# Cutting the A22 weight block last: a reordered weight preparation in a seven-product matmul pipeline

## The chip, the cores and the metric

One core of one Trainium2 chip. The metric is the device time of one execution in microseconds. The kernel runs from instruction streams written out by hand for TensorE (PE), VectorE (DVE), ScalarE (ACT), GpSimd (POOL) and SyncE (SP), which meet only at semaphores; each engine takes its own instructions strictly in order.

## The reference

Two decoder layers over 1024 tokens of width 1024, in float32. Layer 0: RMSNorm with shift and scale from `c`, a gated mixer, a squared-ReLU MLP of width 4096, then one shared key/value projection. Layer 1: stick-breaking attention with 16 heads, then a second MLP.

```python
uv = gelu(h @ w_in); u, v = split(uv); v = _rmsnorm(v, v_norm_g)   # w_in: 1024 x 4096
z = einsum("gts,bnsgc->bntgc", tril(w_s), v) + b_s                 # per chunk of 128 tokens
y = (u * z) @ w_out
...
y = jnp.square(jax.nn.relu(h @ mlp_w_up[layer])) @ mlp_w_down[layer]   # 1024 x 4096, 4096 x 1024
```

Three of these matmuls have the shape (1024 tokens x 1024) by (1024 x 4096): `h @ w_in` and `h @ mlp_w_up` of both layers. The change is about them. They are called stage 0, 1 and 2 below.

## The kernel before

Activations lie transposed, channels on the 128 partitions and tokens along the row. To keep float32 accuracy every operand is kept as two parts in the PE's reduced float format: a high part (`HI`, a copy made by ACT) and a low part (`LO`, the difference, made by DVE). A matmul is then three (`three`, lines 2091 to 2093). Making these two parts is called cutting.

**A stage.** The first 4 of the 32 output tiles (128 channels each) are computed plainly (units `plain`). The other 28 go in 14 pairs of two tiles (`PAIRS`). One pair is a 2 x 2 block matmul (contraction split in two, tokens split in two) done with 7 products in place of 8. The blocks of a pair's weights are

- A1: the upper-left and lower-left quarter together, 128x1024 per cut,
- A22: one quarter, 128x512, read by the seventh product only,
- S1, S2, S3, S4: sums and differences of quarters, 128x512 each, made by `weight_sums` on DVE (lines 1609 to 1614).

The four token blocks T1 to T4 (`T_RAW`, `T_HI`, `T_LO`) are made once per stage. PE runs the products of a pair in the order A1, A1, S2, S1, S3, S4, A22, 12 matmuls of 128x512 each. ACT keeps the first product (`keep`), DVE combines the products: c11 (2 additions, after the third product), c22 (3, after the fifth), c12 (1, after the sixth) and c21 (1, after the seventh), all line 1629. PE waits for c11 before its seventh product, because that one goes to the bank of the third, and for c21 of the pair before at its third product (`made(0)`).

**The pipeline.** While PE works on pair p, ACT and DVE cut the weights of pair p+1 into the other of two weight buffers (`WX`/`WY` for even pairs, `W` for odd ones). The raw weights of one pair lie in a single buffer `RAW` of two 512 KB tiles. SP loads the next pair into it (`load_pair`, line 556) once DVE has counted off the pair's A22 cut. Semaphore `w_lo` counts the cuts in the order of the numbers at line 32 (A1 0, A22 1, S2 2, S1 3, S3 4, S4 5), and every engine's code must cut in that order.

SP's queue also carries, in program order, the stores of the four finished outputs of a pair (`store`, each waits for ACT to finish it) and the loads of modulation weights (`load_mod`, `MODRAW`, 512 KB), each of which waits until DVE has reduced the one before (`mod_reduce`, line 405). Stage 0 has one reduction in each of its first 6 pairs (which also have four additions for a norm, `add_v`), and three or fewer in the others; stage 1 has two in even pairs and one in odd ones; stage 2 has none. At the end of stage 0 the spatial weights `WS_RAW` are loaded; POOL masks them, ACT and DVE cut them in the last pair.

## Time and profile before

| | us |
|---|---|
| median of 3 runs (range) | 2572.84 (2570.56 to 2576.83) |
| the profiled execution, its own time | 2572.84 |
| its span on the engines | 2571.1 |
| PE busy in the span | 2513.3 |
| DVE busy | 1583.1 |
| ACT busy | 995.7 |
| DMA queue q1, share of 16 engines | 41.4% |

1.7 us of the execution lie outside the span. The granted clock of the TensorE was 0.997 on average. A busy time is a union of intervals; matmuls overlap, so a matmul of 390 ns is followed by the next after about 227 ns (12 matmuls, one product, in 2.72 us).

### The profile page before, as it was taken

The numbers are of one execution on the slowest core, as the hardware profiler recorded it, in microseconds if no ns is written. First come the engines' busy times: TensorE is split into PE (matmuls) and PEld (weight loads), VectorE is DVE, ScalarE is ACT, GpSimd is POOL, SyncE is SP. The second block draws the span as 40 slices with busy tenths as digits, with TensorE's granted clock in tenths as the row PEclk, the third lists the DMA queues.
The fourth block names the chain that finished last, engine by engine and source line by source line (L and its number), as shares of the span: only waits on it lengthen the run. The fifth ranks groups of instructions, "written<-read, shape, count | busy, mean of one in ns | idle before, by whom it ended". The sixth has DMA issues, their size and how long they took to land.

```text
span 2571.1 us, 33672 instructions
## 1 busy us (share of the span) xinstructions
PE 2513.3 (98%) x12220; PEld 2053.6 (80%) x12220; DVE 1583.1 (62%) x1907; ACT 995.7 (39%) x1429; POOL 148.9 (6%) x155
## 2 busy tenths in 40 slices
PE   6999999999999999999999999999999999999999
PEld 4888888888888878888898887665788888888887
DVE  6878776668876666666633545777258655444442
ACT  5553343236444431111311335777236444311110
POOL 0000000000000000000000003665000000000000
PEclk9999999999999999999999999999999999999999
DMA  6335573213444475554142264654322322632311
GB/s 255 127 135 180 189 263 121 99 58 126 161 159 151 172 279 185 187 199 139 43 158 82 95 180 131 138 122 113 119 107 107 117 104 106 253 123 82 114 49 66
DMA packets 122981, 359.61 MB, mean 140 GB/s; under 512 B 12032, under 2 KB 28416, under 8 KB 118912
## 3 DMA queue, kind: packets, MB, share of 16 engines
q1 hardware_dynamic: 122880, 358.23, 41.4%
q8 instruction: 67, 1.10, 0.2%
q14 instruction: 34, 0.28, 0.0%
HBM read 270.10 MB, written 88.08 MB: 139 GB/s over the span
## 4 chain that ended last, share of the span: by engine, by line
PE 87%; DVE 6%; ACT 3%; DMA 2%; issue 1%; SPq 0%; ACTq 0%; DVEq 0%
PE PS L2091 25%; PE PS L2092 25%; PE PS L2093 25%; DVE KEEP L2012 2%; PE PS L2612 2%; PE PS L2597 2%; PE PS L2195 1%; PE PS L2197 1%; PE PS L2196 1%; PE PS L2577 1%; PE PS L2498 1%; ACT PS L1314 1%; PE PS L2578 1%; DVE T_RAW L1597 1%; DVE T_LO L1602 1%
## 5 line engine op out<-in xcount | busy, mean ns | idle before, releaser
L2091 PE MATMUL PS<-HID_HI,W_HI 128*128 128x512 f32 x1024 | 400.1, 391 | 5.4 <-DVE HID_LO L1648 5.0
L2093 PE MATMUL PS<-HID_HI,W_LO 128*128 128x512 f32 x1024 | 398.5, 389 | 0.0
L2092 PE MATMUL PS<-HID_LO,W_HI 128*128 128x512 f32 x1024 | 398.4, 389 | 0.0
L395 ACT ACTIVATE W_HI<-RAW 128x1024 fp32r<-128x1024 f32 x114 | 119.5, 1059 | 615.7 <-PE PS L2093 509.6
L1494 DVE SCALAR_TENSOR_TENSOR X<-PS,MODV,X 128x1024 f32<-128x1024 f32 x124 | 159.1, 1283 | 284.0 <-PE PS L2093 275.5
L2091 PE MATMUL PS<-H_HI,W_HI 128*128 128x512 f32 x700 | 277.6, 397 | 4.0 <-DVE H_LO L1438 2.8
L2093 PE MATMUL PS<-H_HI,W_LO 128*128 128x512 f32 x700 | 273.6, 391 | 0.0
L2092 PE MATMUL PS<-H_LO,W_HI 128*128 128x512 f32 x700 | 273.2, 390 | 0.0
L2091 PEld LDWEIGHTS PS<-HID_HI,W_HI 128*128 128x128 f32 x1024 | 192.2, 188 | 49.9 <-DVE HID_LO L1648 7.9
L2093 PEld LDWEIGHTS PS<-HID_HI,W_LO 128*128 128x128 f32 x1024 | 192.2, 188 | 40.0
L2092 PEld LDWEIGHTS PS<-HID_LO,W_HI 128*128 128x128 f32 x1024 | 192.2, 188 | 39.5 <-issue 0.2
L2012 DVE TENSOR_TENSOR_SCAN KEEP<-PS,MASK 128x1024 f32<-128x1024 f32 (+3 forms) x112 | 147.6, 1349 | 47.1 <-ACT PS L1314 38.0
L399 DVE TENSOR_TENSOR W_LO<-RAW,W_HI 128x1024 fp32r<-128x1024 f32 x124 | 150.1, 1218 | 41.7 <-ACT W_HI L1112 24.6
L2091 PEld LDWEIGHTS PS<-H_HI,W_HI 128*128 128x128 f32 x700 | 131.9, 188 | 33.9 <-DVE H_LO L1438 4.3
L405 DVE SCALAR_TENSOR_TENSOR MODRAW<-MODRAW,PS 128x1024 f32<-128x1024 f32 x96 | 116.7, 1216 | 62.4 <-DMA MODRAW<-in_modw 62.1
L2093 PEld LDWEIGHTS PS<-H_HI,W_LO 128*128 128x128 f32 x700 | 131.7, 188 | 28.4
L2092 PEld LDWEIGHTS PS<-H_LO,W_HI 128*128 128x128 f32 x700 | 132.0, 189 | 26.6 <-issue 0.5
L2091 PE MATMUL PS<-T_HI,W_HI 128*128 128x512 f32 x336 | 130.9, 390 | 0.0
L897 POOL TENSOR_TENSOR A<-KEEP 128x1024 f32<-128x1024 f32 (+3 forms) x112 | 126.3, 1147 | 78.6 <-DVE KEEP L2012 77.6
L2093 PE MATMUL PS<-T_HI,W_LO 128*128 128x512 f32 x336 | 130.7, 389 | 0.0
L2092 PE MATMUL PS<-T_LO,W_HI 128*128 128x512 f32 x336 | 130.7, 389 | 0.0
L1629 DVE TENSOR_TENSOR TN<-PS,TN 128x512 f32<-128x512 f32 x147 | 101.3, 689 | 43.2 <-PE PS L2093 38.1
(234 smaller groups left out, 4952.9 us busy)
## 6 DMA issues: line engine op xcount, KB each, us to landing
RAW<-in_wt SPq DMA_DIRECT2D x208, 512.0 KB, 4.0
MODRAW<-in_modw SPq DMA_DIRECT2D x96, 512.0 KB, 3.5
HRAW<-hid_scratch SPq DMA_DIRECT2D x14, 2048.0 KB, 9.1
hid_scratch<-TN SPq DMA_DIRECT2D x90, 256.0 KB, 2.2
hid_scratch<-SCR SPq DMA_DIRECT2D x84, 256.0 KB, 2.2
x_scratch<-X SPq DMA_DIRECT2D x3, 4096.0 KB, 13.8
X<-x_scratch SPq DMA_DIRECT2D x6, 2048.0 KB, 9.2
QK<-qk_scratch SPq DMA_DIRECT2D x16, 768.0 KB, 6.3
```

Of the source, the lines that this page charges most:

```text
L395: act.activation(ring_view(W_HI, n), raw_view(n), ACT.Copy).then_inc(sem["w_hi"], 1)
L399: dve.tensor_tensor(ring_view(W_LO, n), raw_view(n), ring_view(W_HI, n).bitcast(F32), ALU.subtract).then_inc(sem["w_lo"], 1)
L405: dve.scalar_tensor_tensor(MODRAW[:], MODRAW[:], 1.0, flat(CROW), ALU.mult, ALU.mult, accum_out=MODA[:, bass.ds(m.v, 1)]).then_inc(sem["mo ...
L897: pool.tensor_tensor(A[b][:, STRIP[t]:STRIP[t] + w], KEEP[k % 4][:, 0:w], KEEP[k % 4][:, 1:w + 1], ALU.subtract).then_inc(sem["a_ok"], 1)
L1494: dve.scalar_tensor_tensor(X[:, k, :], flat(acc(u % 2)), MODV[:, gate + k:gate + k + 1], X[:, k, :], ALU.mult, ALU.add).then_inc(sem["acc_ ...
L1629: dve.tensor_tensor(HS[x][:, c, :], PS[:, bank, :], HS[x][:, a, :], ALU.add).then_inc(sem["c_made"], 1)
L2012: dve.tensor_tensor_scan(KEEP[k % 4][:, 1:1 + w], strip_scores(k, w), MASK[:, 0:w], 1.0, ALU.mult, ALU.max).then_inc(sem["scanned"], 1)
L2091: pe.matmul(dst, w_hi, m_hi, start=first, stop=False)
L2092: pe.matmul(dst, w_hi, m_lo, start=False, stop=False)
L2093: return pe.matmul(dst, w_lo, m_hi, start=False, stop=last)
L2597: mm = pe.transpose(PS[:, TURNED[n % 3], m * P:(m + 1) * P], block, IDENT[:])
L2612: pe.matmul(PS[r, 6, 0:w], VH[:, b, j, r], AT[q % 3 * 2 + x][:, 0:w], start=(j == KT - 1), stop=(j == 4 * g)).then_inc(sem["av_done"], 1)
```

## The change

The A22 block becomes the last in the cutting order, on ACT, DVE and in the count. Beside that:

- `load_pair`, which waits for the A22 cut, moves down in SP's code: behind the first store and one or two `load_mod` of the pair.
- In a stage's first pair DVE does c11 first, and cuts S2, S1, S3, S4 and A22 only after c21. In the second pair c11 comes ahead of the A1 cut. In all later pairs A22 is cut between S4 and c12.
- `WS_RAW` gets another place (the memory of the even pairs' A22 cut), and is loaded in the next-to-last pair after the seventh product, not at its start.
- In stage 0's last kind of pair one `load_mod` moves ahead of the last store.

```diff
-A1, A22, S2, S1, S3, S4 = range(BLOCKS)
+A1, S2, S1, S3, S4, A22 = range(BLOCKS)
...
-        WS_RAW = at("WS_RAW", [P, GROUPS, CHUNK], F32, RC)
+        WS_RAW = at("WS_RAW", [P, GROUPS, CHUNK], F32, RX + 24 * KB)
...
@@ SP, stages 1 and 2
                 def pair(p, x):
-                    load_pair(p + 1)
                     store(p, 0, 0, 0, 0)
                     if mods:
                         load_mod(sp, p // 2 * 3 + GMODS + 1 + 2 * x)
+                    load_pair(p + 1)
                     if mods and x == 0:
                         load_mod(sp, p // 2 * 3 + GMODS + 2)
...
@@ SP, stage 0
                 def v_pair(p):
-                    load_pair(p + 1)
                     store(p, 0, 0, 0, 0)
                     load_mod(sp, p + 1)
+                    load_pair(p + 1)
                     stores(p)
...
                 def u_pair(p, mods):
-                    load_pair(p + 1)
                     store(p, 0, 0, 0, 0)
                     for n in range(1, min(mods, 2) + 1):
                         load_mod(sp, first + n)
+                    load_pair(p + 1)
                     store(p, 2, 0, 1, 1)
                     store(p, 3, 1, 2, 0)
-                    store(p, None, 1, 3, 1)
                     if mods > 2:
                         load_mod(sp, first + 3)
+                    store(p, None, 1, 3, 1)
...
@@ SP, stage 0, next-to-last pair
                 p = Count(PAIRS - 2)
-                sp.wait_ge(sem["mod_red"], GMODS)
-                sp.dma_start(WS_RAW[:], spw).then_inc(sem["spw_in"], 16)
+                store(p, 0, 0, 0, 0)
                 load_pair(p + 1)
-                store(p, 0, 0, 0, 0)
...
                 store(p, 2, 0, 1, 1)
+                sp.wait_ge(sem["product"], count_of(0, p, PRODUCTS, 7).v)
+                sp.dma_start(WS_RAW[:], spw).then_inc(sem["spw_in"], 16)
...
@@ ACT, start of stages 1 and 2 (of stage 0 and on DVE alike)
                 block_cut(Count(0), 0, A1)
-                block_cut(Count(0), 0, A22)
                 plain(2)
-                for b in (S2, S1, S3, S4):
+                for b in (S2, S1, S3, S4, A22):
                     block_cut(Count(0), 0, b)
...
@@ DVE, pair
+                    second = p.i is None and p.c == 1
+                    if second:
+                        c11(p, x)
                     block_cut(p + 1, 1 - x, A1)
                     weight_sums(p + 1, 1 - x)
-                    block_cut(p + 1, 1 - x, A22)
...
-                    c11(p, x)
+                    if not second:
+                        c11(p, x)
...
                     block_cut(p + 1, 1 - x, S4)
+                    block_cut(p + 1, 1 - x, A22)
                     if kind == "v":
                         add_v(p, 1)
                     c12(p, x)
...
@@ DVE
                 def first_pair():
                     p = Count(0)
+                    c11(p, 0)
                     block_cut(p + 1, 1, A1)
                     weight_sums(p + 1, 1)
-                    block_cut(p + 1, 1, A22)
-                    c11(p, 0)
-                    for b in (S2, S1, S3):
-                        block_cut(p + 1, 1, b)
                     c22(p, 0)
-                    block_cut(p + 1, 1, S4)
                     c12(p, 0)
                     c21(p, 0)
+                    for b in (S2, S1, S3, S4, A22):
+                        block_cut(p + 1, 1, b)
```

DVE, first pair of stage 1, before. `W_LO<-RAW` with 8x128 is the A1 cut and with 4x128 the A22 cut, `S_RAW<-` the sums, `W_LO<-S_RAW` the S cuts, `SCR<-PS,SCR` the combinations of this pair:

```order
L1621 TENSOR_TENSOR W_LO<-RAW,W_HI 128x8x128
L1609 TENSOR_TENSOR S_RAW_107<-RAW 128x4x128
L1610 TENSOR_TENSOR S_RAW_107<-RAW 128x4x128
L1612 TENSOR_TENSOR S_RAW_107<-S_RAW_107,RAW 128x4x128
L1614 TENSOR_TENSOR S_RAW_107<-RAW,S_RAW_107 128x4x128
L1621 TENSOR_TENSOR W_LO<-RAW,W_HI 128x4x128
L1629 TENSOR_TENSOR SCR<-PS,SCR 128x512 x2
L1621 TENSOR_TENSOR W_LO<-S_RAW_107,W_HI 128x4x128 x3
L1629 TENSOR_TENSOR SCR<-PS,SCR 128x512 x3
L1621 TENSOR_TENSOR W_LO<-S_RAW_107,W_HI 128x4x128
L1629 TENSOR_TENSOR SCR<-PS,SCR 128x512 x2
L405 SCALAR_TENSOR_TENSOR MODRAW,MODA<-MODRAW,PS 128x1024 x2
```

The same place in the changed kernel:

```order
L1627 TENSOR_TENSOR SCR<-PS,SCR 128x512 x2
L1619 TENSOR_TENSOR W_LO<-RAW,W_HI 128x8x128
L1607 TENSOR_TENSOR S_RAW_107<-RAW 128x4x128
L1608 TENSOR_TENSOR S_RAW_107<-RAW 128x4x128
L1610 TENSOR_TENSOR S_RAW_107<-S_RAW_107,RAW 128x4x128
L1612 TENSOR_TENSOR S_RAW_107<-RAW,S_RAW_107 128x4x128
L1627 TENSOR_TENSOR SCR<-PS,SCR 128x512 x5
L1619 TENSOR_TENSOR W_LO<-S_RAW_107,W_HI 128x4x128 x4
L1619 TENSOR_TENSOR W_LO<-RAW,W_HI 128x4x128
L405 SCALAR_TENSOR_TENSOR MODRAW,MODA<-MODRAW,PS 128x1024 x2
```

Of the seven additions of the combinations the two of c11 now stand ahead of the A1 cut and the five of c22, c12 and c21 ahead of the S cuts, and the A22 cut stands last, with the modulation reductions still behind it.

DVE, second pair of stage 1, before (`TN<-PS,TN` are its combinations):

```order
L1621 TENSOR_TENSOR WX_LO<-RAW,WX_HI 128x8x128
L1609 TENSOR_TENSOR S_RAW_106<-RAW 128x4x128
L1610 TENSOR_TENSOR S_RAW_106<-RAW 128x4x128
L1612 TENSOR_TENSOR S_RAW_106<-S_RAW_106,RAW 128x4x128
L1614 TENSOR_TENSOR S_RAW_106<-RAW,S_RAW_106 128x4x128
L1621 TENSOR_TENSOR WY_LO<-RAW,WY_HI 128x512
L1629 TENSOR_TENSOR TN<-PS,TN 128x512 x2
L405 SCALAR_TENSOR_TENSOR MODRAW,MODA<-MODRAW,PS 128x1024
L1621 TENSOR_TENSOR WX_LO<-S_RAW_106,WX_HI 128x4x128 x3
L1629 TENSOR_TENSOR TN<-PS,TN 128x512 x3
L1621 TENSOR_TENSOR WX_LO<-S_RAW_106,WX_HI 128x4x128
L1629 TENSOR_TENSOR TN<-PS,TN 128x512 x2
```

And in the changed kernel:

```order
L1627 TENSOR_TENSOR TN<-PS,TN 128x512 x2
L1619 TENSOR_TENSOR WX_LO<-RAW,WX_HI 128x8x128
L1607 TENSOR_TENSOR S_RAW_106<-RAW 128x4x128
L1608 TENSOR_TENSOR S_RAW_106<-RAW 128x4x128
L1610 TENSOR_TENSOR S_RAW_106<-S_RAW_106,RAW 128x4x128
L1612 TENSOR_TENSOR S_RAW_106<-RAW,S_RAW_106 128x4x128
L405 SCALAR_TENSOR_TENSOR MODRAW,MODA<-MODRAW,PS 128x1024
L1619 TENSOR_TENSOR WX_LO<-S_RAW_106,WX_HI 128x4x128 x3
L1627 TENSOR_TENSOR TN<-PS,TN 128x512 x3
L1619 TENSOR_TENSOR WX_LO<-S_RAW_106,WX_HI 128x4x128
L1619 TENSOR_TENSOR WY_LO<-RAW,WY_HI 128x512
L1627 TENSOR_TENSOR TN<-PS,TN 128x512 x2
```

c11 has moved to the front, and the A22 cut (`WY_LO<-RAW`) from behind the sums to behind the S4 cut.

SP, the next-to-last pair of stage 1, before:

```order
L556 DMA RAW<-in_wt 128x1024 x2
L550 DMA hid_scratch<-SCR 128x512
L387 DMA MODRAW<-in_modw 128x1024 x2
L550 DMA hid_scratch<-SCR 128x512 x3
L587 DMA HRAWX<-hid_scratch 128x4x1024
```

And in the changed kernel:

```order
L550 DMA hid_scratch<-SCR 128x512
L387 DMA MODRAW<-in_modw 128x1024
L556 DMA RAW<-in_wt 128x1024 x2
L387 DMA MODRAW<-in_modw 128x1024
L550 DMA hid_scratch<-SCR 128x512 x3
L587 DMA HRAWX<-hid_scratch 128x4x1024
```

The two weight loads stand behind the first store and one modulation load, and ahead of the second modulation load.

## Rows read from the trace of the kernel before

**Rows 1.** Page, part 1: busy us (share of span) and instructions of each engine.
```profile
PE 2513.3 (98%) x12220; PEld 2053.6 (80%) x12220; DVE 1583.1 (62%) x1907; ACT 995.7 (39%) x1429; POOL 148.9 (6%) x155
```

**Rows 2.** Waits of PE, whole span: us in total, times, longest.
```profile
PE PS L2101 <- DVE TOT L1411: 20.1, 1, 20.1
...
PE PS L2091 <- DVE HID_LO L1648: 5.0, 7, 1.6
...
PE PS L2091 <- DVE SCR L1629: 0.8, 2, 0.4
```

**Rows 3.** Stretches: us long, then busy us (x instructions) of each engine, clock, DMA.
```profile
97.00:130.00 33.00, 33.00 (x147) 27.35 (x146) 29.25 (x44) 15.29 (x25) 0.00 (x0) 1.00 0.41 138
```

**Rows 4.** Timeline of PE: start us, us, engine, line, op, [idle before <-releaser].
```profile
90.20 0.39 PE L2091 MATMUL PS<-H_HI,WX_HI 128*128 128x512 f32 x1
...
637.42 0.39 PE L2091 MATMUL PS<-H_HI,WX_HI 128*128 128x512 f32 x1
...
654.29 0.47 PE L2091 MATMUL PS<-T_HI,WY_HI 128*128 128x512 f32 x1 [0.39 <-DVE SCR L1629]
```

**Rows 5.** Timeline of SP, second block.
```profile
856.56 0.90 SPq L556 DMA_DIRECT2D RAW<-in_wt  x2
...
875.51 0.83 SPq L556 DMA_DIRECT2D RAW<-in_wt  x2
```

**Rows 6.** Timeline of DVE, second block, first pair.
```profile
630.52 0.69 DVE L1621 TENSOR_TENSOR WY_LO<-RAW,WY_HI 128x512 fp32r<-128x512 f32 x1
...
646.99 2.29 DVE L1602 TENSOR_TENSOR T_LO<-T_RAW,T_HI 128x2048 fp32r<-128x2048 f32 x1
649.19 1.22 DVE L1621 TENSOR_TENSOR W_LO<-RAW,W_HI 128x1024 fp32r<-128x1024 f32 x1
...
653.46 1.48 DVE L1629 TENSOR_TENSOR SCR<-PS,SCR 128x512 f32<-128x512 f32 x2
...
656.66 2.27 DVE L1629 TENSOR_TENSOR SCR<-PS,SCR 128x512 f32<-128x512 f32 x3
...
665.81 1.22 DVE L405 SCALAR_TENSOR_TENSOR MODRAW<-MODRAW,PS 128x1024 f32<-128x1024 f32 x1 [3.75 <-DMA MODRAW<-in_modw]
```

**Rows 7.** Timeline of DVE, first block, first pair.
```profile
96.54 2.29 DVE L1602 TENSOR_TENSOR T_LO<-T_RAW,T_HI 128x2048 fp32r<-128x2048 f32 x1 [2.03 <-ACT T_HI L1035]
```

**Rows 8.** Timelines of DVE and ACT, second block, a late pair.
```profile
871.12 1.22 DVE L1621 TENSOR_TENSOR W_LO<-RAW,W_HI 128x1024 fp32r<-128x1024 f32 x1 [3.66 <-ACT W_HI L1045]
...
880.37 2.29 DVE L1629 TENSOR_TENSOR SCR<-PS,SCR 128x512 f32<-128x512 f32 x3 [0.54 <-PE PS L2093]
883.26 1.22 DVE L405 SCALAR_TENSOR_TENSOR MODRAW<-MODRAW,PS 128x1024 f32<-128x1024 f32 x1 [0.61 <-DMA MODRAW<-in_modw]
...
870.04 1.57 ACT L1045 ACTIVATE W_HI<-RAW 128x1024 fp32r<-128x1024 f32 x2
```

**Rows 9.** DMA to landing: weight loads all, those at 642, modulation rows 93 to 345.
```profile
DMA to landing us min/median/max: 3.2/4.0/5.5
...
DMA to landing us min/median/max: 4.8/5.2/5.5
...
DMA to landing us min/median/max: 3.2/3.5/4.4
```

**Rows 10.** Stretches after two PE waits, and the first of the waits.
```profile
60.00:63.50 3.50, 3.50 (x10) 2.67 (x10) 2.78 (x5) 3.06 (x5) 0.00 (x0) 0.54 0.00 0
...
953.00:957.00 4.00, 2.47 (x11) 2.05 (x12) 4.00 (x6) 0.00 (x0) 0.00 (x0) 1.00 0.55 155
...
PE PS L2091 <- DVE H_LO L1438: 2.2, 1, 2.2
```

**Rows 11.** Timelines of SP, POOL and ACT around the gate weights.
```profile
321.69 0.34 SPq L679 DMA_DIRECT2D WS_RAW<-in_spw  x1
...
325.35 1.09 POOL L859 TENSOR_SCALAR_AFFINE_SELECT WS_RAW<-WS_RAW 128x1024 f32<-128x1024 f32 x1 [323.01 <-DMA WS_RAW<-in_spw]
...
348.89 1.04 ACT L1206 ACTIVATE H_HI<-WS_RAW 128x1024 fp32r<-128x1024 f32 x1
```

More of the change, by code:

```diff
@@ L1175, in mixer @@
                 block_cut(Count(0), 0, A1)
-                block_cut(Count(0), 0, A22)
                 t_cut(1, 4)
@@ L1179, in mixer @@
                 t_cut(2, 5)
-                for b in (S2, S1, S3, S4):
+                for b in (S2, S1, S3, S4, A22):
                     block_cut(Count(0), 0, b)
@@ L1726, in first_pair @@
                     p = Count(0)
+                    c11(p, 0)
                     block_cut(p + 1, 1, A1)
                     weight_sums(p + 1, 1)
-                    block_cut(p + 1, 1, A22)
-                    c11(p, 0)
-                    for b in (S2, S1, S3):
-                        block_cut(p + 1, 1, b)
                     c22(p, 0)
-                    block_cut(p + 1, 1, S4)
                     c12(p, 0)
                     c21(p, 0)
+                    for b in (S2, S1, S3, S4, A22):
+                        block_cut(p + 1, 1, b)
                     if mods:
@@ L1760, in mlp @@
                 weight_sums(Count(0), 0)
-                block_cut(Count(0), 0, A22)
                 t_sum(3, t_raw(m, 2), t_raw(m, 3), ALU.subtract, 3)
@@ L1771, in mlp @@
                 block_cut(Count(0), 0, S4)
+                block_cut(Count(0), 0, A22)
                 t_cut(4, 4)
@@ L1832, in mixer @@
                 weight_sums(Count(0), 0)
-                block_cut(Count(0), 0, A22)
                 t_cut(2, 2)
                 t_cut(1, 2)
-                for b in (S2, S1, S3, S4):
+                for b in (S2, S1, S3, S4, A22):
                     block_cut(Count(0), 0, b)
```

## The prediction, made before the changed kernel was run

> **What bounds the kernel now.** Read first the busy times: PE is busy for 98% of the span, DVE for 62%, ACT for 39% [rows 1]. Then the list of what PE waited for: the largest entry is 20.1 us before the first product, which the change doesn't touch; in the three stages the change can act on only one kind of wait, 0.4 us each in two stages, on an addition of line 1629 [rows 2]. In a stretch of 33 us in stage 0 PE is busy for all 33.00 us while DVE has 29.25 [rows 3]. So a stage runs at PE's pace, and what DVE, ACT and SP do counts only where it comes later than PE's need. The pace is read from SP: two weight loads 18.95 us apart [rows 5], which is a pair of 7 products of 2.72 us, 19.04 us.
>
> So the question is whether some cut or load, moved later, now passes a date that PE sets. The dates within a pair that begins at 0 are: A1 of this pair at 0, S2 and the c21 of the pair before at 5.44 (third product), c11 of this pair at 16.32 (seventh), A22 at 16.32.
>
> **What is removed.** In stages 1 and 2 the first pair's c11 is late. Stage 1: t_cut 4 ends at 649.3, then DVE cuts A1, makes four sums, cuts A22 and only at 653.46 begins c11, whose product was done at 637.42 + 3 x 2.72 + 0.16 = 645.7 [rows 4, 6]. PE waits 0.39 us for it before its seventh product [rows 4]. With c11 directly behind t_cut 4 it is done at 649.2 + 1.4 = 650.6, and PE wants it at 653.7: the wait goes, twice 0.39 = **-0.8 us**. Late next there is the A22 cut of this pair, which moves from 630.52 to just ahead of t_cut 4 [rows 6]; the DVE work ahead of t_cut 4 is the same in sum, so it is done by 647. Stage 0 has no such wait [rows 2].
>
> **What the moved loads do in the first two pairs.** DVE's durations: A1 1.22, a 512-wide cut, sum or norm addition 0.69, a modulation reduction 1.22, c11 1.48, c22 2.27 [rows 6]; each next one begins some 0.08 before the end of the one before, as 646.99 + 2.29 against 649.19 shows. I count 1.15, 0.60, 1.15, 1.40 and 2.2. A weight load alone lands 3.3 us after issue (minimum 3.2), the second tile some 1.3 later; both after two stores at 642 took 4.8 at least [rows 9].
>
> Stage 0. PE begins at 90.20 [rows 4]; the second pair begins at 109.24, the third at 128.28, and its third product at 133.72. DVE ends t_cut 4 at 96.54 + 2.21 = 98.75 [rows 7], c11 100.15, A1 101.3, sums 103.8, c22 (fifth product done 103.96) 106.3, c12 107.4, c21 (done 109.4) 110.1, five cuts 113.1, reduction 114.25, two norm additions 115.5. SP may now issue the modulation load only at 114.4, and behind it, at 114.8, the weights for pair 2; in the kernel before that load waited for the A22 cut alone, right behind the sums. It lands at 118.1 alone, 119.0 when it goes behind the 512 KB ahead. I take 119.0. ACT copies A1 by 120.1; DVE: c11 119.0, A1 121.3, four sums 123.8, two norm additions 125.1, reduction 126.25, three cuts 128.1, c22 130.3, addition 130.9, S4 and A22 132.1, addition 132.7, c12 133.3, c21 133.95. PE wants it at 133.72: **+0.3 us**. Bounds: 0 if the load lands at once, and +2.5 if it and its sums come 2.2 later, as the slowest landing of a weight load allows (5.5 against 3.3 [rows 9]).
>
> The Trainium skill (DMA: Bandwidth & Descriptors, section on queues, rings and completion order) says that each DMA engine takes the descriptors of one ring in order. The 4.8 us behind the stores agrees with it. By that rule alone the wait is the 0.3 above; without it the term would be 0.
>
> Stage 1. The A22 cut of pair 0 is done at 647.0, so the load of pair 1's weights is issued at 647.2, not at 642.37 as before, and lands at 650.5 and 651.8. DVE: c11 650.6, A1 (ACT at 651.65) 652.8, sums 655.35, c22 657.5, c12 and c21 658.7, five cuts 661.75 (S2 by 659.4; PE's third product of pair 1 begins at 661.9), reduction 662.9. Then comes a wait that stood there before too, for the next modulation load, 3.75 us [rows 6]: reduced at 667.8. Weights for pair 2 issued at 663.4, landed at 667.6. c11 669.2, A1 670.35, sums 672.85, reduction 674.0, three cuts 675.8, c22 678.0, S4 and A22 679.2, c12 and c21 680.4; PE wants it at 675.50 + 5.44 = 680.94: **0**, with 0.5 to spare; +1.7 at the slowest landing. Stage 2 has no reductions, so it is 2 x 1.15 + 3.7 us and another 1.15 earlier: 0.
>
> **All later pairs.** In a late pair of stage 1, ACT copied A1 at 870.04 because `keep` held it until then, not the load, which had been issued at 856.56 [rows 5, 8]. c22 began at 880.37, waiting for PE [rows 8], so c22 stays where it is. The second reduction began at 883.26, when its load had landed [rows 8], and ended at 884.4; S4 takes it to 885.0 and A22, now behind it, to 885.6; the load is issued at 885.7 and lands at 889.0, while the next pair's `keep` lets ACT begin at 870.04 + 19.04 = 889.1. **0**: the load just fits, and it had 10 us more before. Checked as a loop, from A22's end to A22's end: load and issue 3.4, ACT copy 1.1, A1 1.15, sums 2.5, c11 1.4, reduction 1.15, three cuts 1.8, c22 2.2, reduction 1.15, S4 and A22 1.2 = 17.0 us, or about 18.5 where the second reduction waits for its load; a pair of PE lasts 19.04. In stage 0 the three norm additions that fall inside replace one reduction, 17.7. So a lag from the first pairs shrinks by 0.5 to 2 us a pair.
>
> **End of stage 0.** The spatial weights were issued at 321.69 and masked from 325.35, for a use by ACT at 348.89 [rows 11]. Now they go after the seventh product, at 341.6, behind two weight and two V tiles issued from 337.9 on; at 1.3 us a tile they land near 346.9, and are masked by 348.1: 0, with 0.7 to spare; +1.0 if late, since DVE and then PE stand behind that copy. Below zero none of these can go, for PE had no wait to lose there.
>
> **Sum**, against the profiled execution's 2572.84 (a span of 2571.1 and 1.7 around it), which is also the median: -0.8 + 0.3 = -0.5, so 2572.3 us. From no change a measurement of this kernel tells about 0.3%, 7.7 us.
>
> **Rivals.**
> 1. The loop turns longer than PE's pair (slower). It decides from 19.04 us on, that is if loads land 1.5 to 2 us later than now, in all pairs: for it speaks that the load now shares the queue with modulation loads and stores and fits in 889.0 against 889.1; against it, that landings are 4.0 in the median and 5.5 at most with the same traffic [rows 9]. Price: 4.8 for 3.3 makes a loop of 20.0, 1 us over, in 28 pairs of stages 0 and 1, less about 4 us of spare in each: +20, 2592 us.
> 2. The first two pairs slip by their bounds, with the spatial weights: -0.8 + 2.5 + 1.7 + 1.0 = +4.4. A wait above 2 us would also drop PE's clock: after the wait of 2.2 us the granted clock was 0.54, near the lower level of 1.2 GHz, for 3.5 us; after one of 1.6 (in the 5.0 of line 1648) it stayed at 1.00, 2.4 GHz [rows 2, 10]. Half speed in such a stretch costs half of it, 1.7. Together +6, 2579. The skill says the same (TensorE: Matmul & The Clock Gate, section on why this matters for your kernels): gaps between bursts of matmuls bring back the half clock. With waits of 0.3 us the sum is not changed by it.
> 3. Nothing moves: the waits of 0.39 stay in another form, for instance on A22 of pair 0. 2572.8.
> 4. Faster by more than 7.7 us: all that PE waits for in the stages is 0.8 us [rows 2]; only a faster matmul could do it, and nothing here changes one.
>
> **Chances.** Forecast (-0.5, within 2 us) 0.60, rival 3 0.15, rival 2 0.14, rival 1 0.08, rival 4 0.03. The range of 8 in 10 takes the forecast, the spread of the three runs (2570.6 to 2576.8) and most of rival 2: 2569 to 2579. Slower by over 0.3%: rival 1 and a little of rival 2, 0.10; faster 0.04; within 0.3% 0.86.
>
> **What would show it.** PE's list of waits without the 0.4 us entries on line 1629's additions at the seventh product of the first pairs, and with at most one short new one, near 134 us, at a third product. Weight loads issued just behind the S4 and A22 cuts, about 10 us later in each pair. In the middle of a stage 33.00 us of PE in 33. It is wrong if PE waits in the pairs of the loops (rival 1), or if the spatial weights' mask holds ACT near 349.

## The result, and the profile after

| | before | changed |
|---|---|---|
| median of 5 runs (range) | 2572.84 (2570.56 to 2576.83) | 2584.97 (2584.76 to 2593.39) |
| profiled execution | 2572.84 | 2585.84 |
| its span | 2571.1 | 2584.1 |

The ratio is 1.0054, with a 95% interval of 1.0036 to 1.0072. The kernel is slower by 12 us by the medians, 13 in the profiled executions and 14 by the ratio, where 2572.3 had been forecast and 2569 to 2579 given as the range.

The busy times of the page say nothing of it; they are those of [rows 1] within 3 us, PE even a little less:

```profile
PE 2512.6 (97%) x12220; PEld 2053.3 (79%) x12220; DVE 1583.3 (61%) x1907; ACT 993.1 (38%) x1429; POOL 149.0 (6%) x155
```

So nothing became longer; something waits. Here is what PE waited for between 95 and 900 us of the span, that is in stage 0, behind it and in stage 1 (engine, tile, line <- releaser: us in total, times, longest). In the kernel before this stretch had the 0.39 of line 1629, 0.5 on line 1523 and 0.3 on line 993 and nothing else above 0.25:

```profile
PE PS L2090 <- DVE TN L1627: 5.0, 4, 1.6
PE PS L2090 <- DVE H_LO L1521: 4.0, 1, 4.0
PE PS L2455 <- DVE S_RAW L1723: 2.1, 1, 2.1
PE PS L2271 <- DVE V_IN L1515: 1.3, 1, 1.3
PE PS L2090 <- DVE SCR L1627: 0.5, 1, 0.5
PE PS L2295 <- ACT SCR L993: 0.3, 1, 0.3
```

DVE's lines are 2 lower than before and PE's 1 lower: L1627 is the combination that was L1629. ACT's copy of the weights is L1045 in both, its later copy L1206 is now L1204. The single waits, from PE's timeline: 1.32 us at 133.17 (third product of the third pair), 1.48 at 287.31, 0.51 at 307.15, 1.64 at 328.37 (third products of stage 0's late pairs), 2.12 at 343.50, 1.29 at 357.68, 3.98 at 365.51, and in stage 1 a single 0.56 at 694.92. The two waits of 0.39 us [rows 4] are gone, as forecast.

The stretches answer to [rows 3] and show the place (us long, then busy us and instructions of PE, PEld, DVE, ACT, POOL, then clock, DMA share, GB/s). The middle of the stage's first half is as full as it was; the stretch of the pairs with three modulation reductions is not, though DVE has less to do in it than PE; and the last stretch stands right behind the wait of 3.98:

```profile
97.00:130.00 33.00, 33.00 (x147) 27.33 (x146) 26.16 (x41) 13.38 (x23) 0.00 (x0) 1.00 0.31 104
224.00:330.00 106.00, 102.36 (x448) 83.57 (x447) 77.17 (x120) 35.14 (x58) 0.00 (x0) 1.00 0.58 182
366.00:369.50 3.50, 3.50 (x16) 3.11 (x15) 3.24 (x5) 1.11 (x1) 0.00 (x0) 0.51 1.06 371
```

In the kernel before, the second stretch has 106.00 of 106. The next view tells why. These are the weight loads (`RAW`) issued between 222 and 330 us, twelve tiles, in the changed kernel; in the kernel before the same view of the same stretch says 3.2/4.0/5.3 (over all of its weight loads it was 3.2/4.0/5.5 [rows 9]) and names nobody who waited:

```profile
who waited for it (us, times):
  ACT WX_HI L1045: 11.7, 3
  ACT W_HI L1045: 9.9, 3
...
DMA to landing us min/median/max: 5.4/6.2/7.9
```

One pair of them, on SP, DVE and ACT (start us, us, engine, line, op, [idle before <-releaser]):

```profile
223.59 0.35 SPq L387 DMA_DIRECT2D MODRAW<-in_modw  x1
224.80 0.86 SPq L556 DMA_DIRECT2D RAW<-in_wt  x2
226.06 1.16 SPq L550 DMA_DIRECT2D hid_scratch<-SCR  x2
228.30 0.35 SPq L387 DMA_DIRECT2D MODRAW<-in_modw  x1
...
245.12 0.86 SPq L556 DMA_DIRECT2D RAW<-in_wt  x2
```

```profile
223.94 0.68 DVE L1619 TENSOR_TENSOR W_LO<-RAW,W_HI 128x512 fp32r<-128x512 f32 x1
...
230.76 1.06 ACT L1045 ACTIVATE WX_HI<-RAW 128x1024 fp32r<-128x1024 f32 x1 [3.59 <-DMA RAW<-in_wt]
...
231.86 1.23 DVE L1619 TENSOR_TENSOR WX_LO<-RAW,WX_HI 128x1024 fp32r<-128x1024 f32 x1 [3.73 <-ACT WX_HI L1045]
...
244.26 0.68 DVE L1619 TENSOR_TENSOR WY_LO<-RAW,WY_HI 128x512 fp32r<-128x512 f32 x1
```

A22 ends at 224.6, the load goes out at 224.80, ACT can begin at 230.76, 5.94 us later, DVE's A1 at 231.86, and the next A22 ends at 244.9: a loop of 20.3 us. The six loads of these pairs are issued at 224.80, 245.12, 265.05, 286.03, 305.73 and 326.85, so the loop takes 19.7 to 21.1 us, 20.4 on average, against PE's 19.04. DVE falls behind PE by 1.4 us a pair, PE's reserve lasts for three pairs, and then it waits.

A second, smaller part of the loop is DVE's wait for the second modulation load of a pair, 0.4 to 1.15 us in four of the five loops:

```profile
283.42 1.22 DVE L405 SCALAR_TENSOR_TENSOR MODRAW<-MODRAW,PS 128x1024 f32<-128x1024 f32 x1 [1.15 <-DMA MODRAW<-in_modw]
```

In the kernel before only the third reduction of a pair waits in these pairs (0.8 to 1.2 us), ahead of A1. The new waits are not enough by themselves: with the old landing of 3.3 us in place of 6.0 on average, the loop would be 17.7 us by this estimate, waits included.

The end of stage 0, on SP, POOL, ACT, DVE and PE, which answers to [rows 11]:

```profile
346.86 0.81 SPq L556 DMA_DIRECT2D RAW<-in_wt  x2
347.87 0.89 SPq L659 DMA_DIRECT2D V_IN<-hid_scratch  x2
...
349.33 0.47 SPq L688 DMA_DIRECT2D WS_RAW<-in_spw  x1
...
359.49 1.09 POOL L859 TENSOR_SCALAR_AFFINE_SELECT WS_RAW<-WS_RAW 128x1024 f32<-128x1024 f32 x1 [357.15 <-DMA WS_RAW<-in_spw]
...
360.61 1.06 ACT L1204 ACTIVATE H_HI<-WS_RAW 128x1024 fp32r<-128x1024 f32 x1 [4.89 <-POOL WS_RAW L859]
...
356.21 1.42 DVE L1515 SCALAR_TENSOR_TENSOR V_IN<-V_IN,VGC,V_TOT 128x512 f32<-128x512 f32 x2 [7.25 <-DMA V_IN<-hid_scratch]
...
365.51 0.39 PE L2090 MATMUL PS<-H_LO,H_HI 128*128 128x256 f32 x1 [3.98 <-DVE H_LO L1521]
```

The spatial weights land 10.0 us after issue (at 349.33), the V tiles 8.3 and 9.2 us after theirs; ACT, DVE and PE stand behind them one after the other.

**The account.** In this paragraph the same matmul is taken from both traces. At the wait for ACT's `HP` (68.33 us before, 66.30 changed) the changed kernel is 2.0 us ahead, since this execution kept its full clock at 60 us and that of before did not [rows 10]. At the first wait behind stage 1 (905.01 and 918.46) it is 13.45 us behind. So 15.5 us were lost between the two. The list has 13.7 of them. New waits up to 366 us, with what stood there before taken off, are 1.32 + 1.48 + 0.51 + 1.64 + 2.12 + 1.29 + (3.98 - 0.49) = 11.85. The half clock behind the last one costs 1.7. Stage 1 has 0.56 more and the removed 0.39 less. The other 1.8 us lie in gaps too short for the list, 0.1 to 0.2 us at each new wait and its neighbours. Behind 905 us the gains and losses nearly cancel, 13.0 at the end: stage 2 loses its 0.39, a wait of 1.2 on line 1492 (at 1119 us) is new where one of 0.35 on that line at 940 has gone, and of the two traces only that of before has a stretch at half clock at 1265 us. No run ties these to the change.

### The profile page after: what moved, and what is told of

Read it like the earlier page. It is cut to its first block, busy times and chain, and to the rows that moved or that the text cites. A ratio compares the mean times of both kernels' runs of the same rounds, so it can differ in the third digit from the quotient of the medians.

```text
span 2584.1 us, 33672 instructions
## 1 busy us (share of the span) xinstructions
PE 2512.6 (97%) x12220; PEld 2053.3 (79%) x12220; DVE 1583.3 (61%) x1907; ACT 993.1 (38%) x1429; POOL 149.0 (6%) x155
## 4 chain that ended last, share of the span: by engine, by line
PE 78%; DVE 8%; DMA 6%; ACT 3%; issue 3%; SPq 1%; DVEq 0%; ACTq 0%; POOL 0%; POOLq 0%
PE PS L2090 22%; PE PS L2092 22%; PE PS L2091 22%; DMA RAW<-in_wt 2%; DMA MODRAW<-in_modw 2%; DVE KEEP L2011 2%; PE PS L2596 2%; PE PS L2611 2%; PE PS L2194 1%; PE PS L2576 1%; PE PS L2195 1%; PE PS L2196 1%; PE PS L2497 1%; PE PS L2577 1%; ACT PS L1312 1%
## 5 line engine op out<-in xcount | busy, mean ns | idle before, releaser
L1627 DVE TENSOR_TENSOR TN<-PS,TN 128x512 f32<-128x512 f32 x147 | 101.3, 689 | 42.6 <-PE PS L2092 36.6
```

Source lines behind the costliest of these rows:

```text
L1627: dve.tensor_tensor(HS[x][:, c, :], PS[:, bank, :], HS[x][:, a, :], ALU.add).then_inc(sem["c_made"], 1)
```

## Experiments

Theory A from here on: a weight load with a modulation load just ahead of it and stores behind it lands late, and with A22 cut last its landing is part of a loop that has no time to spare; the spatial weights come on top. The rivals change from run to run and stand in the expectations. "Before" is measured again in each group of runs.

**1. The second modulation load behind the weights.** The changed kernel, in stage 0's three-reduction pairs:

```diff
-                    for n in range(1, min(mods, 2) + 1):
-                        load_mod(sp, first + n)
+                    load_mod(sp, first + 1)
                     load_pair(p + 1)
+                    load_mod(sp, first + 2)
```

> The changed kernel with one edit: in the last 6 pairs of stage 0 that carry three modulation loads (two in the last of them) the second modulation load is issued behind the two weight loads, not 1.2 us ahead of them. In the changed kernel those weight loads land 5.5 to 7.0 us after issue (3.3 in the other pairs). Theory A (a modulation load just ahead slows the weight load, and so makes the loop from A22 cut to A22 cut longer than PE's 19.04 us): the weight tiles land after 3.3 to 3.8 us, the waits of PE at the third product (1.5, 0.5, 1.6 us) and for the norm's diagonal (2.1 us) go, the waits behind them shrink by some 2 us; 7 to 8 us less than the changed kernel, 2577 us. Theory B (the stores issued behind the weight load slow it): they still land after 5.5 us or more, and the time stays at 2585.

Measured: 2597.92 us against 2571.21, ratio 1.0110 (1.0093 to 1.0127): 13 us worse than the changed kernel, which neither theory had said. The first half of A holds, the first tile lands in 3.2 to 3.35 us again. But the modulation loads now queue behind the weights, and DVE, in its fixed order, stands at the third reduction before the next A1:

```profile
225.30 1.48 DVE L1627 TENSOR_TENSOR SCR<-PS,SCR 128x512 f32<-128x512 f32 x2
233.22 1.22 DVE L405 SCALAR_TENSOR_TENSOR MODRAW<-MODRAW,PS 128x1024 f32<-128x1024 f32 x1 [6.43 <-DMA MODRAW<-in_modw]
```

The second modulation load, issued 1.1 us behind the weights, takes 6.5 us to arrive. That makes the loop 21.8 to 22.2 us. This order only moves the lateness from one load of the pair to another.

**2. The spatial weights at their old place.** The changed kernel with `WS_RAW` in its old memory and its load ahead of the next-to-last pair's first store:

```diff
-        WS_RAW = at("WS_RAW", [P, GROUPS, CHUNK], F32, RX + 24 * KB)
+        WS_RAW = at("WS_RAW", [P, GROUPS, CHUNK], F32, RC)
...
                 p = Count(PAIRS - 2)
+                sp.wait_ge(sem["mod_red"], GMODS)
+                sp.dma_start(WS_RAW[:], spw).then_inc(sem["spw_in"], 16)
                 store(p, 0, 0, 0, 0)
...
-                sp.wait_ge(sem["product"], count_of(0, p, PRODUCTS, 7).v)
-                sp.dma_start(WS_RAW[:], spw).then_inc(sem["spw_in"], 16)
```

> The changed kernel with the spatial weights back at their old place and time (issued at the start of stage 0's next-to-last pair, when the last modulation reduction is done). In the changed kernel they land 10.0 us after issue, the POOL mask ends at 360.6 us and PE waits 4.0 us for the first spatial matmul. Theory A (that landing is what PE waits for): the wait falls from 4.0 to about 1.2 us, since the V tiles, still late, bound it next; 2.8 us less than the changed kernel, about 2583 us in the profiled run. Theory B (the V tiles, landed after 8.3 and 9.2 us, are what bounds it): the wait stays near 4 us, and the time at 2585.8.

Measured: 2577.28 us (one execution), 8.6 less than the changed kernel's profiled one. PE's waits from 95 to 900 us:

```profile
PE PS L2090 <- DVE TN L1627: 3.5, 4, 1.5
PE PS L2455 <- DVE S_RAW L1723: 1.7, 1, 1.7
PE PS L2090 <- DVE H_LO L1521: 0.9, 1, 0.9
...
```

3.98 has become 0.95, and the half clock behind it is gone; that is 4.7. The rest of the 8.6 lies in smaller waits before it (1.1 less in the late pairs, 0.9 at 343 and 357), and in parts that the edit doesn't touch. Run 7 gives the edit's price with more executions.

**3. Both edits.** The changed kernel with the diffs of 1 and 2.

> Both edits together: second modulation load behind the weight loads in stage 0, spatial weights early. If both mechanisms are what costs, only the wait of 1.3 us in stage 0's third pair and small ones are left: 2574 to 2576 us. If the loop is too long for another reason (DVE's own work), 2580 or more.

Measured: 2596.58, ratio 1.0105 (1.0088 to 1.0122). The expectation of 2574 to 2576 failed. The loop stays too long, but for run 1's reason, the late modulation load, and not for DVE's own work. The spatial weights' wait is 0.49 as before, and 4.40 us stand at 346.74 instead.

**4. Stores out of the way.** The changed kernel, with SP waiting, behind the weight loads, until DVE has cut A1 of the weights being loaded. The first store behind them no longer waits for ACT, and the third modulation load is held back with the stores:

```diff
                     load_pair(p + 1)
-                    store(p, 2, 0, 1, 1)
+                    sp.wait_ge(sem["w_lo"], blocks_cut(0, p + 2, A1).v)
+                    sp.dma_start(HIDD[(p * 2 + 4).v, :, half_of(1)], HS[p % 2][:, 1, :]
+                                 ).then_inc(sem[f"hs_out{p % 2}"], 16)
                     store(p, 3, 1, 2, 0)
```

> The changed kernel, modulation load still ahead of the weight loads in stage 0, but the three stores (and the third modulation load) behind the weight loads wait until DVE has cut the A1 block of those weights, so nothing is issued in the 5 us after them. Theory A (the load ahead slows them): the weight tiles still land after 5.5 us or more, time 2585 or a little over, as the third modulation load comes later. Theory B (what is issued behind them slows them): they land after 3.3 to 3.8 us, the waits of PE at the third products go, 2578 to 2580 us.

Measured: 2583.75 (one execution). The twelve tiles from 222 to 330 us (in the changed kernel 5.4/6.2/7.9):

```profile
DMA to landing us min/median/max: 4.1/5.3/6.4
```

The first tiles land in 4.1 to 4.5 us, one in 5.58, where neither theory had them. So part of the delay goes when nothing is issued behind the load, and part stays. The time hardly follows, since the third modulation load is now late and DVE waits for it 1.3 to 2.0 us in each loop:

```profile
279.52 1.22 DVE L405 SCALAR_TENSOR_TENSOR MODRAW<-MODRAW,PS 128x1024 f32<-128x1024 f32 x1 [2.04 <-DMA MODRAW<-in_modw]
```

The loads are 20.2 us apart on average, and waits of 0.65, 1.11, 0.25 and 0.46 stand at third products from 268 to 328 us.

**5. Small modulation loads.** The changed kernel with

```diff
-            sp.dma_start(MODRAW[:], modw[(j + MOD_FIRST).v]).then_inc(sem["mod_in"], 16)
+            w = slice(0, P) if small(j) else slice(0, D)
+            sp.dma_start(MODRAW[:, w], modw[(j + MOD_FIRST).v][:, w]).then_inc(sem["mod_in"], 16)
...
-            dve.scalar_tensor_tensor(MODRAW[:], MODRAW[:], 1.0, flat(CROW), ALU.mult, ALU.mult,
+            dve.scalar_tensor_tensor(MODRAW[:], MODRAW[:], 0.0 if small(j) else 1.0, flat(CROW), ALU.mult, ALU.mult,
```

`small(j)` is true for the modulation loads of stage 0 that stand in its pairs.

> The changed kernel, but each modulation load of stage 0 brings 64 KB (128 of 1024 columns) in place of 512 KB; DVE's reductions stay as long as they were (left out: seven eighths of each of these loads, and their values count as zero). Theory A (the weight loads land late because of the modulation load just ahead of them and the stores behind): in pairs with three reductions the first weight tile lands 4.1 to 4.6 us after issue in place of 5.5 to 7.0, the loop from A22 cut to A22 cut is back to PE's 19.0 us, and the waits of 1.48, 0.51 and 1.64 us at the third products of the late pairs are gone; the spatial weights' wait of 3.98 us shrinks to 2 to 3; 2580 to 2582 us. Theory B (it is DVE's own work, three reductions and the cuts in one row behind the load, that makes the loop long): landings may fall, but the loop stays at 20 us or more and the three waits stay; 2584 to 2586 us.

Measured: 2576.83 against 2572.54, ratio 1.0017 (1.0008 to 1.0027). The loads of the three-reduction pairs land 3.25 to 3.87 us after issue, faster than A had said, and the loop follows them (SP, two pairs; lines here are 4 higher than in the changed kernel):

```profile
223.92 0.86 SPq L560 DMA_DIRECT2D RAW<-in_wt  x2
241.89 0.86 SPq L560 DMA_DIRECT2D RAW<-in_wt  x2
```

18.0 us in place of 20.3, with the same reductions and cuts on DVE. From the third load on the loads are 18.9 to 19.7 us apart, with DVE waiting for PE. PE's waits from 95 to 900 us:

```profile
PE PS L2094 <- DVE H_LO L1525: 3.1, 1, 3.1
PE PS L2094 <- DVE TN L1631: 1.4, 2, 0.8
...
```

Nothing is left at 287, 307, 328, 343 and 357 us. Theory B (DVE's own work makes the loop long) is out. This takes 9.5 us off the changed kernel's ratio (0.0037 x 2572), and a wait of 3.1 us for the spatial weights stays. The small loads also end DVE's waits for the modulation weights inside the loop. In the first loop, which had none, the load-to-A1 part alone went from 7.06 to 4.64 us, so the landing suffices to bring the loop under 19.04.

**6. The change in stages 1 and 2 only.** A22's place in the cutting order, SP's order and c11's place depend on the stage:

```diff
+ORDER = ((A1, A22, S2, S1, S3, S4), (A1, S2, S1, S3, S4, A22), (A1, S2, S1, S3, S4, A22))
...
+                    if m == 0:
+                        block_cut(p + 1, 1 - x, A22)
...
                     block_cut(p + 1, 1 - x, S4)
+                    if m:
+                        block_cut(p + 1, 1 - x, A22)
```

> The change in stages 1 and 2 alone: there A22 is cut last, the weight loads stand behind the first store and modulation load, and c11 is first in the first pair and first in the second. Stage 0 and the spatial weights are as in the kernel before. Theory A (the whole loss is in stage 0): stage 0 without new waits, the waits of 0.39 gone, one of 0.56 us at the third product of stage 1's third pair; 2571.2 - 0.8 + 0.6 = 2571.0 us, equal to the kernel before within 1.5 us. Rival (the later cut of A22 costs in every stage, a part of the 13 us being lost in many gaps too short to be listed): 2574 us or more.

Measured: 2571.23 against 2572.54, ratio 0.9997 (0.9988 to 1.0006). From 95 to 900 us PE's waits are one of 0.62 at stage 1's third pair and the two behind stage 0 that the kernel before has. This trace alone has a wait of 2.72 us on line 1496 at 942 us, where before had 0.35; its own execution, 2575.78, is the slowest of eleven. The loss is in stage 0 and its end.

**7. Both causes out.** Kernel 5 with edit 2.

> The changed kernel with both suspects out: each modulation load of stage 0 brings 64 KB in place of 512 KB (left out as in the kernel with small modulation loads before), and the spatial weights are loaded at their old place, ahead of the next-to-last pair's first store. Theory A (late landings in the three-reduction pairs and the late spatial weights are all that the change costs beyond the first pair): left are 0.6 us at the third product of stage 0's third pair and 0.8 in stage 1; no wait over 1 us between 280 and 370 us; 2571.5 to 2573.5 us. Rival (a third cause): 2575 us or more, with waits near 343, 357 and 361 us.

Measured: 2571.78 against 2572.04, ratio 1.0001 (0.9992 to 1.0011). Waits from 95 to 900 us:

```profile
PE PS L2094 <- DVE TN L1631: 1.7, 2, 1.4
PE PS L2094 <- DVE H_LO L1525: 0.5, 1, 0.5
...
```

So of the changed kernel's 0.0054, 0.0037 go with the large modulation loads (give or take 0.002), 0.0016 or 4.1 us with the spatial weights (0.0013), and 0.0001 is left (0.001). No third cause is needed. Of the expected remainders, 0.6 at stage 0's third pair and 0.8 in stage 1, came 0.28 and 1.42.

**8. SP's order alone.** The kernel before, with the three moves of `load_pair` in SP's code and nothing else; A22 is still cut right behind the sums. In stage 0's three-reduction pairs:

```diff
-                    load_pair(p + 1)
                     store(p, 0, 0, 0, 0)
                     for n in range(1, min(mods, 2) + 1):
                         load_mod(sp, first + n)
+                    load_pair(p + 1)
```

> The kernel before with the change's order on SP alone: the weight loads stand behind the first store and the modulation loads of the pair in all three stages; A22 is still cut right behind the sums, and the spatial weights and c11 are as before. Theory A (a load that lands late costs only where the cuts behind it have no time left; it is the A22 cut ahead of it that closes the loop): in stage 0's pairs with three reductions the loads are issued behind the second modulation load, some 9 us later than before and 2 to 3 us earlier than in the changed kernel, and land 5 to 6.5 us after that; from the second modulation load on the loop is about 19 us, PE's own pace; at most one or two waits under 1 us at third products; 2571 to 2574 us. Rival (SP's order alone is the cause, the place of the A22 cut plays no part): waits of 0.5 to 1.6 us at 287, 307 and 328 us as in the changed kernel, 2575 us or more.

Measured: 2572.64 against 2572.04, ratio 1.0000 (0.9991 to 1.0009). SP's weight loads, and in the second fence who waited for the twelve tiles from 222 to 330 us and how long they took:

```profile
226.91 0.86 SPq L556 DMA_DIRECT2D RAW<-in_wt  x2
246.28 0.86 SPq L556 DMA_DIRECT2D RAW<-in_wt  x2
...
```

```profile
  ACT W_HI L1045: 11.2, 6
  ACT WX_HI L1045: 8.3, 3
...
DMA to landing us min/median/max: 4.8/5.9/6.9
```

The loads are issued late, land late (first tiles 4.8 to 5.4 us, in the changed kernel 5.45 to 7.0), and ACT waits about as long for them, but PE hardly notices:

```profile
PE PS L2091 <- DVE TN L1629: 0.6, 1, 0.6
PE PS L2091 <- DVE H_LO L1523: 0.5, 1, 0.5
PE PS L2091 <- DVE SCR L1629: 0.4, 1, 0.4
...
```

So SP's order alone is not the cause. But the reason in theory A, that the A22 cut ahead closes the loop, is not what the trace shows. Here too the loop is closed: the load stands behind the second modulation load, which waits for DVE's second reduction, and ACT waits for every weight load:

```profile
251.33 1.06 ACT L1045 ACTIVATE W_HI<-RAW 128x1024 fp32r<-128x1024 f32 x1 [2.68 <-DMA RAW<-in_wt]
```

The loop takes 18.6 to 19.4 us, 19.0 on average: it just fits PE's 19.04, with nothing to spare. The changed kernel's is 1.4 us longer. From issue to A1 it has 0.8 us more (7.1 against 6.3), and 0.6 more from A1 to the next issue, nearly all of it DVE's waits inside the loop, which are absent here but for one of 0.3. Without these waits the stretch is 12.7 us in both: the load comes 1.5 us behind the second reduction there and 0.9 here, but here the 0.6 of the A22 cut stand ahead of c11. What A22's last place costs at equal landings no run shows, and why the landings are 0.9 us shorter here stays open.

**9. The first pair with its cuts at the old places.** The changed kernel with S2, S1, S3 ahead of c22 and S4, A22 ahead of c12 in the first pair:

```diff
                     weight_sums(p + 1, 1)
+                    for b in (S2, S1, S3):
+                        block_cut(p + 1, 1, b)
                     c22(p, 0)
+                    for b in (S4, A22):
+                        block_cut(p + 1, 1, b)
                     c12(p, 0)
                     c21(p, 0)
-                    for b in (S2, S1, S3, S4, A22):
-                        block_cut(p + 1, 1, b)
```

> The changed kernel, but in a stage's first pair DVE cuts S2, S1, S3 ahead of c22 and S4, A22 ahead of c12, so that the load for the third pair is issued some 2 us earlier. Theory A (each wait in stage 0 is DVE's lag behind PE, which the first pair starts and the loop with late loads adds to): the wait of 1.32 us at 133 us is under 0.3, those of 1.48, 0.51 and 1.64 stay or come one pair later with about the same sum, since the loop is longer than PE's pair in either case; the wait of 0.56 in stage 1 is gone; 2584 to 2585.5 us against 2585.8. Rival (the first pair starts the lag and the later pairs only carry it on): the waits at 287, 307 and 328 us go as well, 2580 us or less.

Measured: 2584.15 against 2572.54, ratio 1.0046 (1.0030 to 1.0061). The wait at 133 us is gone, those at 287, 307 and 328 are 1.39, 0.77 and 1.02: the late pairs make their own lag, as A says (2584.15, inside its range). Stage 1 did the opposite of what was expected, 1.40 and 0.32 us where 0.56 had been.

**10 and 11. c11 first and nothing else.** The kernel before with

```diff
                     p = Count(0)
+                    c11(p, 0)
                     block_cut(p + 1, 1, A1)
                     weight_sums(p + 1, 1)
                     block_cut(p + 1, 1, A22)
-                    c11(p, 0)
```

> The kernel before with one edit: in the first pair of stages 1 and 2 (and of stage 0, which uses the same code in another order only where it says so) c11 is done ahead of the A1 cut. Nothing else of the change. Theory A (all of the loss comes from the A22 cut being last, c11's place gives 0.8 us): the two waits of 0.39 us on the additions of the combinations are gone, weight loads land in 3.2 to 3.5 us in stage 0 as before, no new waits; 0.8 us under the kernel before, 2570.4 us. Rival (c11's place costs something of its own, since the A1 cut and the sums behind it come 1.5 us later): a new wait of 0.3 to 1.5 us at the third product of the second pair, 2571 to 2573 us.

> The kernel before with c11 ahead of the A1 cut in a stage's first pair, once more, on another occasion, since its first comparison gave 2570.01 against 2572.54 us, with an interval that ends at 0.9999. Theory A (only the two waits of 0.39 us go): a ratio of 0.9997, 0.5 to 1 us below the kernel before. Rival (the spatial weights, the weight ring or an alignment of later waits gain 2 us more each time): 2 to 3 us below again.

Measured: 2570.01 against 2572.54, ratio 0.9990 (0.9981 to 0.9999), and 2569.67 against 2572.04, ratio 0.9988 (0.9979 to 0.9997). Up to 900 us PE waits only twice:

```profile
PE PS L2091 <- DVE H_LO L1523: 0.5, 1, 0.5
PE PS L2296 <- ACT SCR L993: 0.3, 1, 0.3
```

The two waits of 0.39 are gone and no others came. This version beats both, faster than before by a tenth of a per cent, and than the changed kernel by about 15 us. The gain is 2.5 us the first time and 2.4 the second. That is the rival's "2 to 3 us below again" and not theory A's 0.5 to 1. Each interval alone just reaches the 0.9997 that 0.8 us make; two such results together speak for more. PE's waits in the stages have nothing that would account for it, so where the other 1.6 us come from is open.

## Why the prediction was wrong, step by step

- **What is removed: right in mechanism.** The waits of 0.39 us went, and no A22 cut took their place; runs 10 and 11 show it alone, with 1.6 us more than the term of 0.8.
- **First two pairs: near.** 0.3 us had been forecast and 1.32 came, inside the bound of 2.5. Everything in this trace is 2.0 us early, since the stage began at 88.17 and not at 90.20. Counted from there, the load was issued 0.3 us later than in the working (113.06, for 114.8) and landed 4.84 us after that (4.2 were taken). These two make the 1.0 us missed. Stage 1's 0 was 0.56 (bound 1.7).
- **All later pairs: the step that failed.** "The load just fits" held in stage 1, as the rows below this point show, which answer to [rows 5, 8]. The load goes out 6.1 us ahead of DVE's A1 and lands in 3.4, and ACT copies it right behind `keep`. There the modulation load stands 2.5 us or more ahead from the third weight load on, and all of those land in 3.1 to 3.5 us. Stages 1 and 2 lost nothing that run 6 could measure. The step failed in stage 0's three-reduction pairs. The prediction has no loop for these. Its 17.7 is for the pairs with norm additions, and 17.0 to 18.5 for two reductions, with "load and issue 3.4". The terms measured from 224.6 on are these: issue 0.2, landing 5.94, ACT's copy 1.1, A1 and sums 3.7, c11 with 0.5 between its additions 1.75, and to the end of A22 7.6, which is 20.3. The third reduction costs nothing, for it falls into the landing. So of the 3.3 us above 17.0, 2.7 are the landing and 0.5 a wait inside c11; in the later loops the wait for the second modulation load stands in place of the latter. The landing had been taken from loads with nothing issued just ahead of them: in the kernel before, the weights were loaded right behind the A22 cut, 4.4 us or more behind the last modulation load. The prediction used the price of a transfer in its old place for its new one. Where it did price the queue (4.2, 4.8) it was for the first pairs alone.

```profile
878.45 0.88 SPq L556 DMA_DIRECT2D RAW<-in_wt  x2
...
883.00 0.60 ACT L1049 ACTIVATE SCR<-PS 128x512 f32<-128x512 f32 x1 [0.76 <-PE PS L2092]
883.49 1.05 ACT L1045 ACTIVATE W_HI<-RAW 128x1024 fp32r<-128x1024 f32 x1
...
884.57 1.23 DVE L1619 TENSOR_TENSOR W_LO<-RAW,W_HI 128x1024 fp32r<-128x1024 f32 x1 [3.67 <-ACT W_HI L1045]
```

- **Rival 1 named the mechanism**, the load that shares the queue, and got 0.08. Its loop of 20.0 is near the measured 20.4 partly by luck: it took 18.5 and a landing of 4.8, where 17.0 and landings of 5.45 to 7.0 would have been right. The reason against it, "landings are 4.0 in the median and 5.5 at most with the same traffic", was not a reason: the bytes were the same, their order in the queue was not. Its price of 20 us assumed 28 pairs; it was six loads of stage 0, and 9.5 us went when they landed early (run 5).
- **End of stage 0: mis-sized.** The landing was put at 346.9 and the bound at +1.0. The load could only be issued at 349.33, behind weights that waited for the A22 cut until 346.86, and it took 10.0 us, with two weight tiles, two V tiles and a store issued in the 2.5 us ahead of it. With the V tiles late as well (8.3 and 9.2 us; 3.9 and 4.8 before), the copy began at 360.61, 11.7 us later than before, when PE itself was 8.2 us late, and PE stood for 3.98. The term was 4.1 us (run 7 against run 5, give or take 3), half clock included; the traces of the two agree, with a wait of 3.12 against 0.49 and 1.7 for the half clock.
- **"Below zero none of these can go"** is right as far as PE's waits show it, while the 1.6 us of runs 10 and 11 stay open.

The largest error was in the chances: 0.10 for slower by over 0.3%, when the change gave up 10 us of reserve in each pair, a fact the prediction names, for 0.8 us.

## What to carry to other kernels

When a load is moved behind other transfers, its old time to landing is no longer its price: look at what is issued just ahead of it and behind it at the new place (here 1.2 us), pair by pair, and take a row of a load that stands so. Then close the loop, buffer free, load, copy, cut, buffer free, with that price for each kind of iteration, not for the common one. Here a slack of 2 us in 19 was not enough. And check whether the part of the edit that removes the wait can be had without the part that spends the reserve: here it could.

## What the runs showed of the hardware

**Landing of a 512 KB weight tile**, the first of two, in stage 0, all on one queue. A store is 256 KB; rows without a remark are of the three-reduction pairs.

| what is issued around it | us to landing |
|---|---|
| before: nothing just ahead, a store 2 us and a modulation load 2.6 us behind | 3.2 to 3.5 |
| changed, pairs with one reduction: 512 KB 5.6 us ahead, stores from 1.4 us behind | 3.2 to 3.35 |
| changed: 512 KB 1.2 us ahead, stores from 1.3 us and in most 512 KB 3.5 us behind | 5.45 to 7.0 |
| run 4: 512 KB 1.2 us ahead, nothing behind for 5 us | 4.1 to 4.5, one 5.6 |
| run 5: 64 KB 1.2 us ahead, stores and 64 KB behind | 3.25 to 3.9 |
| run 1: no load just ahead, 512 KB 1.1 us and stores behind | 3.2 to 3.35 |
| run 8: 512 KB 0.5 us ahead, stores from 1.2 us behind | 4.8 to 5.4 |
| run 8, pairs with one reduction: a store and 512 KB 0.6 us ahead, nothing behind for 5 us | 4.5 to 5.0, one 5.8 |

In these rows no tile is late without 512 KB within 1.2 us ahead of it. With that load, 0.8 to 2.5 us are added when nothing is issued behind, and 1.5 to 3.7 when something is. A store just ahead counts too: loads right behind two stores landed in 4.8 to 5.5 us in the kernel before (those at 642, [rows 9]). What stands behind adds nothing by itself. Run 4 against the changed kernel says that it adds to the lateness, but run 8's two rows differ little, so how much it adds is not settled. The Trainium skill (DMA: Bandwidth & Descriptors, section on queues, rings and completion order) says that a DMA engine takes descriptors in ring order, but that the semaphore's increment lands only after every earlier write of that engine. What is ahead can delay a load by that rule, and run 4 agrees with its 1 us. That section states nothing by which what is issued behind should delay it. The cause below the queue stays open; no run here looked at it.

**The clock.** In six traces PE waited 3.1 to 4.8 us at or behind stage 0's end, and each time the granted clock fell to the lower level, for 3.4 us (as in the third stretch above, 0.51) or for 6.8. It fell too after the 2.60 us of run 1 at 377 us and the 2.72 of run 6 at 942. After the wait of 2.15 us at 59 us, which stands in all 13 traces, it fell in five and stayed in eight. The waits of 2.12 at 343.50 in the changed kernel and 2.10 at 133.79 in run 4 were not followed by a drop. So the prediction's "above 2 us" was no threshold. PE's program up to 59 us is the same in all 13, and the five (before, runs 3, 6, 8 and 9) share no edit. So executions can differ by 1.7 us for this alone.
